# One-hot matrices of the second key taken through DRAM scratch, with the auxl residuals held behind the rows on GpSimd

## The reference, cut to what matters

```python
sv, si = lax.top_k(sc, PEER_TOPK)
cand = sv[:, :, 0, :, None] + sv[:, :, 1, None, :]
cv, ci = lax.top_k(cand.reshape(PEER_CHUNK, PEER_HEADS, PEER_TOPK * PEER_TOPK), PEER_TOPK)
i1 = jnp.take_along_axis(si[:, :, 0], ci // PEER_TOPK, axis=-1)
i2 = jnp.take_along_axis(si[:, :, 1], ci % PEER_TOPK, axis=-1)
e = i1 * PEER_NKEYS + i2
g = jax.nn.softmax(cv.astype(jnp.float32), axis=-1)
act = jax.nn.gelu(jnp.einsum('td,thkd->thk', xc, u[e]))
return jnp.einsum('thk,thkd->td', g * act, v[e])
```

## Time and profile before

| | us |
|---|---|
| median of three runs | 1135.31 |
| range of these runs | 1131.75 to 1135.49 |
| the profiled execution, its own time | 1133.95 |
| its span in the profile | 1132.1 |
| PE busy | 1098.9 |
| DVE busy | 899.5 |
| ACT busy | 700.6 |
| GpSimd (POOL) busy | 276.0 |

### The profile page before, as it was taken

One profiled execution on the slowest core, in us unless ns is written; L12 is line 12 of the kernel. 1 busy time (PEld: TensorE's weight loads), 2 busy tenths in 40 slices (PEclk: granted clock), 3 DMA queues, 4 the chain that ended last, 5 costly groups with the idle time before them and its releaser, 6 DMA issues.

```text
span 1132.1 us, 22243 instructions
## 1 busy us (share of the span) xinstructions
PE 1098.9 (97%) x7174; PEld 978.1 (86%) x7174; DVE 899.5 (79%) x1701; ACT 700.6 (62%) x1234; POOL 276.0 (24%) x260
## 2 busy tenths in 40 slices
PE   6999999998999999999999999999999999999998
PEld 5788888798999999999999999877777777888887
DVE  5745666575899998889999999999999998444444
ACT  4345556665344444457777777798988886454543
POOL 0000222100000212653333333222222222545453
PEclk9999999998999999999999999999999999999999
DMA  7464222264445555545444444444444445555553
GB/s 253 158 218 147 75 91 77 76 197 162 162 143 176 168 189 186 188 160 167 152 163 155 160 158 157 149 136 150 151 149 151 146 154 201 191 192 197 187 198 115
DMA packets 50016, 181.34 MB, mean 160 GB/s; under 512 B 5552, under 2 KB 5680, under 8 KB 49968
## 3 DMA queue, kind: packets, MB, share of 16 engines
q1 hardware_dynamic: 49968, 180.72, 47.3%
HBM read 178.60 MB, written 2.10 MB: 160 GB/s over the span
## 4 chain that ended last, share of the span: by engine, by line
PE 52%; DVE 22%; issue 21%; ACT 2%; DVEq 2%; DMA 1%; POOL 0%; SPq 0%; POOLq 0%; ACTq 0%
PE bank L679 16%; DVE gsum L1441 7%; DVE lo L1311 4%; DVE big L1449 4%; PE bank L628 4%; PE bank L322 4%; PE bank L629 4%; PE bank L630 4%; PE bank L323 3%; PE bank L324 3%; PE bank L571 1%; DVE same L1423 1%; DMA raw<-wpre_d 1%; PE bank L336 1%; PE bank L337 1%
## 5 line engine op out<-in xcount | busy, mean ns | idle before, releaser
L925 ACT ACTIVATE hi<-raw 128x1024 fp32r<-128x1024 f32 x253 | 268.1, 1060 | 257.3 <-PE bank L630 151.3
L1311 DVE TENSOR_TENSOR lo<-raw,hi 128x1024 fp32r<-128x1024 f32 x253 | 315.2, 1251 | 105.4 <-ACT hi L925 104.6
L628 PE MATMUL bank<-xhi,hi 128*128 128x256 f32 x1024 | 294.1, 287 | 0.8 <-DVE lo L1311 0.8
L629 PE MATMUL bank<-xlo,hi 128*128 128x256 f32 x1024 | 289.9, 283 | 0.0
L630 PE MATMUL bank<-xhi,lo 128*128 128x256 f32 x1024 | 289.8, 283 | 0.0
L1554 POOL TENSOR_TENSOR auxl<-big,auxh 128x256 fp32r<-128x256 f32 x128 | 138.1, 1079 | 267.9 <-ACT auxh L960 267.9
L628 PEld LDWEIGHTS bank<-xhi,hi 128*128 128x128 f32 x1024 | 196.4, 192 | 2.2 <-issue 1.1
L629 PEld LDWEIGHTS bank<-xlo,hi 128*128 128x128 f32 x1024 | 196.6, 192 | 0.0
L630 PEld LDWEIGHTS bank<-xhi,lo 128*128 128x128 f32 x1024 | 196.2, 192 | 0.0
L679 PE MATMUL bank<-hi,auxh 128*128 128x512 f32 x508 | 161.3, 399 | 2.5 <-ACT hi L925 2.2
L679 PE MATMUL bank<-lo,auxh 128*128 128x512 f32 x508 | 158.0, 392 | 0.0
(11 more groups left out here) (236 smaller groups left out, 1726.5 us busy)
## 6 DMA issues: line engine op xcount, KB each, us to landing
raw<-u_d SPq DMA_DIRECT2D x128, 512.0 KB, 3.3
raw<-v_d SPq DMA_DIRECT2D x128, 512.0 KB, 3.2
raw<-wpre_d SPq DMA_DIRECT2D x78, 512.0 KB, 3.9
big<-x_d SPq DMA_DIRECT2D x2, 512.0 KB, 3.7
out_d<-big SPq DMA_DIRECT2D x2, 512.0 KB, 5.0
big<-out_d SPq DMA_DIRECT2D x2, 512.0 KB, 4.9
out_d<-big SPq DMA_DIRECT2D x4, 256.0 KB, 2.1
big<-cst_d SPq DMA_DIRECT2D x1, 719.5 KB, 7.8
```

The lines of the kernel that those rows point to most:

```text
L628: pe.matmul(out, wh, xhi[:, k, :], start=(k == 0), stop=False)
L629: pe.matmul(out, wh, xlo[:, k, :], start=False, stop=False)
L925: act.activation(hi[:, n % SPLIT, :], raw[:, n % RING, :], ACT.Copy).then_inc(hi_done, 1)
L1311: dve.tensor_tensor(lo[:, n % SPLIT, :], raw[:, n % RING, :], hi[:, n % SPLIT, :].bitcast(F32), ALU.subtract).then_inc(lo_done, 1)
```

## The change

- Three slots of `oneB` in place of two (SLOTS). To make room, `same` has one slot in place of two, and the weights g lie in `gsum` in place of a third part of `eT` until they are used.
- Each low group's finished `oneB` (128 x 512, 256 KB) is stored by SP to a scratch tensor `ob_d` in DRAM (`save_b`), between the fetches of tiles. For each high group SP loads it back (`load_b`), AHEAD = 5 steps ahead in the program's order; `load_b` of a group waits until the group three before it has left its slot. ACT's `one_hot_b` is gone, and PE's high groups wait for the load (`ob_in`).
- GpSimd's `distances` waits as before for the group two back, and also until the store of the slot's last content has ended (`ob_saved`).
- SP's stream of tiles is cut at LEAD = 7 tiles, so that stores and loads stand between the right fetches.
- `keys_equal` runs two groups ahead in place of three.
- GpSimd's `w_lo` of v tiles 3 to 63 waits, besides for `auxh`, until `rows_a` of group 64 + tile number has ended (`w_lo_behind_rows`).

The core of the diff (the rest is `% 2` made into `% SLOTS`, and the calls that start and end the loops):

```diff
@@ SP
-            stream(u_d, N_PRE, 0, NBLK)
-            stream(v_d, N_PRE + NBLK, 0, HALF)
+            def fetch(src, first, at_, i, j):
+                sp.wait_ge(lo_done, i * UNROLL + splits(first + at_ + j - RING + 1))
+                load((first + at_ + j) % RING,
+                     src[bass.ds(i * UNROLL + (at_ + j), 1)].rearrange("a p c -> (a p) c"))
+            def save_b(i, j, base):
+                g = base + j
+                sp.wait_ge(S("oneB_ready"), i * UNROLL + (g + 1))
+                sp.dma_start(ob_d[bass.ds(i * UNROLL + g, 1)].rearrange("a p c -> (a p) c"),
+                             oneB[:, g % SLOTS, :, :].rearrange("p t k -> p (t k)").bitcast(F32)
+                             ).then_inc(ob_saved[g % SLOTS], 16)
+            def load_b(i, j, base):
+                g = base + j
+                sp.wait_ge(S("g_ready"), i * UNROLL + (NGRP + g - SLOTS + 1))
+                sp.dma_start(oneB[:, g % SLOTS, :, :].rearrange("p t k -> p (t k)").bitcast(F32),
+                             ob_d[bass.ds(i * UNROLL + g, 1)].rearrange("a p c -> (a p) c")
+                             ).then_inc(ob_in[g % SLOTS], 16)
+            def fetch_and_save(i, j):
+                save_b(i, j, 1)
+                fetch(u_d, N_PRE, HALF + LEAD, i, j)
+            def fetch_and_load(i, j):
+                load_b(i, j, AHEAD)
+                fetch(v_d, N_PRE + NBLK, LEAD, i, j)
+            stream(u_d, N_PRE, 0, HALF + LEAD)
+            save_b(0, 0, 0)
+            each_tile(sp, HALF - LEAD, fetch_and_save)
+            for j in range(LEAD - 1):
+                save_b(0, j, HALF - LEAD + 1)
+                fetch(v_d, N_PRE + NBLK, 0, 0, j)
+            fetch(v_d, N_PRE + NBLK, 0, 0, LEAD - 1)
+            for q in range(SLOTS):
+                sp.wait_ge(ob_saved[q], 16 * len(range(q, NGRP, SLOTS)))
+            for g in range(AHEAD):
+                load_b(0, g, 0)
+            each_tile(sp, HALF - LEAD, fetch_and_load)
+            for j in range(HALF - LEAD + AHEAD, NGRP):
+                load_b(0, 0, j)
@@ PE, g_group
-                pe.wait_ge(S("oneB_ready"), i * UNROLL + (g + 1))
+                if g < NGRP:
+                    pe.wait_ge(S("oneB_ready"), i * UNROLL + (g + 1))
+                else:
+                    pe.wait_ge(ob_in[(g - NGRP) % SLOTS], i * (16 * UNROLL // SLOTS) + 16 * ((g - NGRP) // SLOTS + 1))
@@ ACT: one_hot_b and its calls removed
-                one_hot_b(i, j, NGRP + 2)
                 loop_hi(i, V0 + j + SPLIT)
                 w_hi(i, j + SPLIT)
@@ DVE, group_step
-                    keys_equal(i, j, base + 3)
+                    keys_equal(i, j, base + 2)
@@ POOL
-                if g >= 2:
+                if g >= SLOTS:
                     pool.wait_ge(S("g_ready"), i * UNROLL + (g - 1))
+                    pool.wait_ge(ob_saved[g % SLOTS], i * (16 * UNROLL // SLOTS) + 16 * (g // SLOTS))
...
-            each_tile(pool, NBLK, lambda i, j: w_lo(i, j))
+            def w_lo_behind_rows(i, j):
+                pool.wait_ge(S("oneA_ready"), i * UNROLL + (NGRP + SPLIT + j + 1))
+                w_lo(i, SPLIT + j)
+            for b in range(SPLIT):
+                w_lo(0, b)
+            each_tile(pool, HALF - SPLIT, w_lo_behind_rows)
+            each_tile(pool, HALF, lambda i, j: w_lo(i, HALF + j))
```

More of the change, by code:

```diff
@@ L61 @@
 SPLIT = 3
+SLOTS = 3
+LEAD = 7
+AHEAD = 5
 UNROLL = 12
@@ L201, in build @@
         kep_in = sem("kep_in")
+        ob_saved = [sem(f"ob_saved{q}") for q in range(SLOTS)]
+        ob_in = [sem(f"ob_in{q}") for q in range(SLOTS)]
         hi_done = sem("hi_done")
@@ L981, in _ @@
             act.wait_ge(S("bank67_read"), 2)
-            act.activation(gw2[:, :, 0], eT[:, 2, :], ACT.Copy).then_inc(S("gw2_hi"), 1)
+            act.activation(gw2[:, :, 0], gw_, ACT.Copy).then_inc(S("gw2_hi"), 1)
             fold_b(0, 0, 0)
@@ L986, in _ @@
             each_tile(act, HALF - 1, u_step_g)
-            one_hot_b(0, 0, NGRP)
             act.wait_ge(S("weighed"), 1 + NGRP)
@@ L1429, in rows_a @@
                 dve.wait_ge(S("same"), i * UNROLL + (g + 1))
-                eq_ = same[:, g % 2, :, :].unsqueeze(2).broadcast_to([P, 4, 2, HALF])
+                eq_ = same[:, :, :].unsqueeze(2).broadcast_to([P, 4, 2, HALF])
                 w_ = gw2[:, bass.ds(i * (4 * UNROLL) + 4 * (g % NGRP), 4), :].bitcast(F32)
@@ L1451, in _ @@
             dve.wait_ge(S("gw2_hi"), 1)
-            link(dve.tensor_tensor(gw2[:, :, 1], eT[:, 2, :], gw2[:, :, 0].bitcast(F32), ALU.subtract))
-            keys_equal(0, 0, 0)
-            keys_equal(0, 1, 0)
-            rows_a(0, 0, 0)
-            keys_equal(0, 2, 0)
-            rows_a(0, 1, 0)
+            link(dve.tensor_tensor(gw2[:, :, 1], gw_, gw2[:, :, 0].bitcast(F32), ALU.subtract))
+            for g in range(2):
+                keys_equal(0, g, 0)
+                rows_a(0, g, 0)
             for j in range(ROUTER, HALF):
@@ L1490, in _ @@
             for j in range(NGRP - 4, NGRP - 1):
-                group_step(0, j, NGRP + 1, keys=False, rows=j == NGRP - 4)
+                group_step(0, j, NGRP + 1, keys=j == NGRP - 4, rows=j == NGRP - 4)
                 loop_lo(0, V0 + j + SPLIT)
@@ L1537, in distances @@
                 g = base + j
-                if g >= 2:
+                if g >= SLOTS:
                     pool.wait_ge(S("g_ready"), i * UNROLL + (g - 1))
+                    pool.wait_ge(ob_saved[g % SLOTS], i * (16 * UNROLL // SLOTS) + 16 * (g // SLOTS))
                 i2 = eT[:, 1, bass.ds(i * (4 * UNROLL) + 4 * g, 4)].unsqueeze(2).broadcast_to([P, 4, P])
-                pool.tensor_tensor(oneB[:, g % 2, :, :], iota.unsqueeze(1).broadcast_to([P, 4, P]), i2,
+                pool.tensor_tensor(oneB[:, g % SLOTS, :, :], iota.unsqueeze(1).broadcast_to([P, 4, P]), i2,
                                    ALU.subtract).then_inc(S("dist"), 1)
             pool.wait_ge(S("bank67_read"), 2)
-            distances(0, 0, 0)
-            distances(0, 1, 0)
-            each_tile(pool, NGRP - 2, lambda i, j: distances(i, j, 2))
+            for g in range(SLOTS):
+                distances(0, g, 0)
+            each_tile(pool, NGRP - SLOTS, lambda i, j: distances(i, j, SLOTS))
             V0 = N_PRE + NBLK
```

41 lines of the change are left out of this document (16 added, 25 removed).

## The result

| | before | after |
|---|---|---|
| median (runs shown) | 1135.0 us (1131.75 to 1135.49) | 1157.28 us (1154.79 to 1159.25) |
| profiled execution, time / span | 1133.95 / 1132.1 us | 1159.25 / 1157.4 us |
| granted clock, mean | 0.994 | 0.987 |

The medians are those of four runs of each kernel; the kernel before has one more run here than ahead of the prediction. The changed kernel takes 1.0201 times as long, 95% interval 1.0173 to 1.0229: it is slower, by 1.7 to 2.3%, and the forecast was 1121.2 us, faster. The high half and the passage to it came out as forecast. Nearly the whole miss lies in the low half, where the prediction had priced the stores at nothing.

The account below looks back on a forecast made before the run. PE bounds two stages; in the high half DVE, held up by GpSimd, sets 3.513 us a step against PE's 3.20. Sum: 1133.95 - 19.1 (high half) + 6.3 (first load) = 1121.2 us, range 1114 to 1129.

Parts of the forecast that it names:

- High half: High half: with GpSimd's `auxl` behind the rows, DVE's step falls to 3.02 us, PE paces at 3.20: -19.1 us.
- ACT's relief: High half: four squares and a relu leave ACT, busy 0.90 of the time; counted as room, 0 us.
- the remark in brackets: High half: had ACT kept its work, its own waits could have taken DVE's place; no size given.
- First load: Passage to the high half: load of group 64 queues behind a waiting fetch; PE pauses, clock drops: +6.3 us (4.1 to 8.0).
- the row that the forecast went by: Trace's other long pause: PE stood 4.3 us, full clock came 5.0 us after the restart, 2.5 us lost.
- Loads of the high half and the end: High half: loads asked three steps (9.6 us) ahead, 3.2 to 5.0 suffice; end still waits for `auxl`: 0 each.
- Stores in the low half: Low half: 64 stores of 256 KB have 6.2 us to land, traffic fits, PE's step stays 3.31 us: 0.
- DMA cannot keep up: Rival, low half: stores land much later than 6.2 us or transfers fill the engines; about 1134 us, chance 0.04.
- The lock moves: Rival, high half: GpSimd starts first and holds `lo` up to 0.6 us; no gain, 1140.3 us, chance 0.06.
- half of the relief: Rival, high half: GpSimd still costs DVE half; step 3.26 to 3.37 us, about 1131 to 1127 us, chance 0.08.
- Start of the groups: Start: three distances made ahead in place of two, first rows one `same` earlier; a few tenths of either sign.

Follow-up runs that it names:

- The run with held distances: Changed kernel, stores as late as they were, GpSimd's low-half distances also waiting for DVE's `rows_a` of the same step: 1124.25 us, ratio 0.9915 to the kernel before.
- the stores that nobody waits for: Changed kernel with all 64 stores made from another buffer, `xhi`, and no distances waiting for them: 1122.39 us (one execution).

## Why the prediction was wrong

**High half: right.** Forecast 3.20 us a step and -19.1 us over 61; measured 3.207 and -18.6 over 60. `keys_equal` 0.42, `auxl` 1.37 from inside a `lo`, no wait of PE's weight loads for `oneA`: each as written. The runs with and without the wait bear out the mechanism. They do not bear out how the gain was shared: the prediction gave all of it to GpSimd's wait and 0 to ACT's relief, but the wait alone brings 0.13 of the 0.31 us a step, and the rest comes only with ACT's one-hots gone, as the remark in brackets allowed.

**First load: right in kind, and to the tenth by luck.** Forecast +6.3 us, measured +6.3 (14.21 to 20.53). The pause was 8.55 us in place of 7.5 to 8, with the clock of 0.50 behind it, and the load's landing ended it. Group 64 came 8.6 us later after group 63 than before, in place of the forecast 7.9; from there to group 67 PE made up 2.3 us, in place of 1.6, as the low clock lasted some 4 us (0.50 from 772 to 774 us, 0.54 to 776, 1.00 from there) where the row that the forecast went by had 5.0. The two misses of 0.7 us cancel. With the stores one step earlier the pause was 7.98 us, so some 0.5 us of it belongs to the late stores.

**Loads of the high half and the end: right** at 0; after group 127 the two profiles differ by 0.1 us.

**Stores in the low half: wrong, and it is nearly the whole miss.** Forecast 0, measured +31.0 us of the stretch's +32.5 (the other 1.5 are its first step, below). The step that failed is the sentence that "GpSimd takes the slot again in the distances two steps after the row at 600.79, at 607.4", with a slack of 6.2 us. Two things were wrong in it:

- The count of steps. DVE adds up a group while PE already runs the next one: in the trace of before PE starts group 26 at 600.05, and DVE's sum of group 25 starts at 600.80. I had counted the store by DVE's group and GpSimd by PE's, as if they were one. If the store issued at about 601.2 is that of group j + 1, the distances at 600.79 are those of group j + 3, and the next ones, of group j + 4, already take the store's slot: one step later, at 604.1. The slack is 2.9 us. The run with stores one step earlier fits it: a single step was enough. The one-hots of that store were ready at 599.18, not at 599.67: the relus before lie 2.83 and 3.80 us apart in turns and not 3.31, which made no difference here.
- The landing. I took 2.1 us from the 256 KB stores of the earlier trace rows. These are the last four transfers of the kernel, 0.6 to 0.7 us apart, with no fetch ahead of them; 0.6 us behind a fetch a store took 3.9 (median of 64 in the profile after). I had 5.0 as the upper bound, and it "fits" only against 6.2.

By these numbers either error alone would have done no harm: 601.2 + 2.1 = 603.3 is before 604.1, and 601.2 + 3.9 = 605.1 is before 607.4. Together they make the release late by 1 us; in the changed kernel the distances start 2.15 us after PE has begun the group that would free them (median), where it was 0.74 before, 1.4 us later. This late release became 0.54 us of a step only because it moved GpSimd from beside `add_parts` and `keys_equal`, where it cost 0.3 us, to just ahead of `rows_a`, `lo` or `weigh`, where it costs 0.85. The run with held distances shows that.

**The rivals.** "DMA cannot keep up" had the right place and sign with the wrong cause: it wanted stores later than 6.2 us or engines that are full, and a chance of 0.04. The traffic was harmless, as the stores that nobody waits for show. "The lock moves" had the right mechanism at the wrong place: I looked for the collision in the high half, at `lo`, and it came in the low half, at `rows_a` in 39 of 60 steps and at `lo` in 10. No rival had a low half in which GpSimd's start is moved. The text said that "GpSimd's distances keep their place, and `keys_equal` its 0.72 us" and gave no bound for the case that they do not; `keys_equal` at 0.41 in the low half was a sign that they had moved. The row for that bound was at hand: the earlier trace rows shows 0.48 us a step for a collision, and over 60 steps that is 29 us. The rival "half of the relief" has a slip in its sum: steps of 3.26 to 3.37 us give about 1125 to 1132 us, not 1127 to 1131.

**Start of the groups.** I gave "a few tenths of either sign". Group 0 to group 1 takes 4.91 us in the changed kernel and 3.42 in the one before (513.80 to 517.22), and 0.5 us more is lost ahead of group 0, so this was 2.0 us.

## What to carry to other kernels

When a transfer's end frees a buffer, count the steps from issue to reuse by the group numbers of one engine, never across engines that run one group apart, and price the landing as it is behind the transfer ahead of it in the queue. Where two engines exclude each other at a port, any new wait that moves the start of one needs a price for the row it will meet next, even if the wait itself seems to have slack: here a start moved by 1.4 us cost 0.54 us in every step, and a wait that sets who goes first won it back. Two relief measures on engines that are both near the limit are to be tried together before one is judged, as neither shows its full worth alone (0.13 and 0 us a step here, 0.31 together).

## What was unexpected of the hardware

- A 256 KB store landed in a median of 3.9 to 4.0 us when issued 0.6 us behind a 512 KB fetch, and in 2.4 us when issued 1.5 to 2.1 us behind one; the runs with held distances and with the stores one step earlier have the same step of 3.31 us and the same bytes in it. In both a store landed 0.7 to 0.9 us (medians) after the fetch ahead of it had landed, though one was issued 1.2 us later behind it than the other. So here the price of such a store is that of the fetch and 0.7 to 0.9 us more, counted from the fetch's issue. Four stores in a row with no fetch ahead had 2.1 us. By the Trainium skill's page "DMA: Bandwidth & Descriptors", section "Anatomy of one DMA" (a fit for transfers issued by GpSimd), it would be 2.6 us, an estimate; the stores without a fetch close ahead (2.1 and 2.4 us) lie a little under it, and those behind one well above.
- GpSimd's distances, 1.04 us alone, took 1.92 us beside DVE's `lo` of 1.23, and a `lo` beside them took 2.06. What each loses depends on who starts first, and a lead of 0.05 us was enough.
- Stores a step later still left the low half's step at 3.85 us, with the same rows held but ACT and PE waiting for the one-hots.
- Ahead of the groups the same code had a spread of 6.4 us from one profiled execution to another (group 0 at 512.54 and 518.98). It goes with the granted clock of TensorE. Summed over the windows of 10 us up to 510 us, what the clock lacked to full speed is 3.4 us in the earliest of the thirteen and 10.2 us in the latest; from 210 to 220 us, for example, PE was granted 0.70 in the profile of the changed kernel and 1.00 in that of the kernel before. What sets it apart from one execution to the next, no run here shows.
